# FFN opening product: every second weight unit as seven block products instead of eight

## The reference, cut to what matters

```python
h = rmsnorm(x, norm_ffn)                    # (512, 1024)
gt, up = jnp.split(h @ w_ffn_in, 2, axis=-1)  # w_ffn_in: (1024, 2 * 2816)
x = x + (jax.nn.silu(gt) * up) @ w_ffn_out  # w_ffn_out: (2816, 1024)
return rmsnorm(x, norm_final)
```

## Time and profile before

| what | value |
|---|---|
| runs of the kernel before | 799.06, 799.15, 800.95 us, median 799.15 |
| profiled execution | 799.31 us, its span 797.5 us |
| TensorE busy | 789.9 us of the span (99%) |
| VectorE, ScalarE, GpSimd busy | 406.2 us, 290.0 us, 24.8 us |
| granted TensorE clock, mean | 0.999 of full speed |
| HBM traffic | 75.34 MB read, 3.19 MB written |

### The profile page before, as it was taken

How to read it: one execution, slowest core, us unless ns; L and a number is a source line. 1 busy time by engine, 2 the same in 40 slices (tenths; PEclk the granted TensorE clock), 3 DMA queues, 4 the chain that set the end, 5 groups by cost and what they waited for, 6 DMA issues and landing times.

```text
span 797.5 us, 11178 instructions
## 1 busy us (share of the span) xinstructions
PE 789.9 (99%) x4382; PEld 659.1 (83%) x4382; DVE 406.2 (51%) x816; ACT 290.0 (36%) x524; POOL 24.8 (3%) x36
## 2 busy tenths in 40 slices
PE   9999999999999999999999999999999999999996
PEld 7878899889878787888889888888888888888885
DVE  5935333556766776656518533444433444422347
ACT  6112155243647666643317221222221223222235
POOL 1301000000000000003100000000000000000000
PEclk9999999999999999999999999999999999999999
DMA  7931354330311111164231333322333321222202
GB/s 236 345 116 53 106 102 137 83 110 4 106 53 54 54 55 41 40 185 133 105 106 54 106 105 105 102 77 84 105 105 105 102 87 75 106 105 105 105 1 106
DMA packets 100216, 79.08 MB, mean 99 GB/s; under 512 B 16929, under 2 KB 94801, under 8 KB 100177
## 3 DMA queue, kind: packets, MB, share of 16 engines
q1 hardware_dynamic: 99936, 78.26, 32.9%
q10 hardware_dynamic: 240, 0.29, 0.1%
HBM read 75.34 MB, written 3.19 MB: 98 GB/s over the span
## 4 chain that ended last, share of the span: by engine, by line
PE 99%; DMA 0%; ACT 0%; DVE 0%; issue 0%; ACTq 0%; DVEq 0%
PE bank L1451 28%; PE bank L1452 28%; PE bank L1453 28%; PE bank L1684 2%; PE bank L1703 2%; PE bank L1671 2%; PE bank L1585 1%; PE bank L1626 1%; PE bank L1607 1%; PE bank L1548 1%; PE bank L1475 1%; PE bank L1492 1%; PE bank L1698 1%; PE bank L1498 0%; PE bank L1501 0%; PE bank L1638 0%
## 5 line engine op out<-in xcount | busy, mean ns | idle before, releaser
L1451 PE MATMUL bank<-h_hi,w_hi 128*128 128x512 f32 (+1 forms) x368 | 140.0, 380 | 0.0
L1452 PE MATMUL bank<-h_lo,w_hi 128*128 128x512 f32 (+1 forms) x368 | 139.8, 380 | 0.0
L1453 PE MATMUL bank<-h_hi,w_lo 128*128 128x512 f32 (+1 forms) x368 | 139.8, 380 | 0.0
L1451 PE MATMUL bank<-n_hi,w_hi 128*128 128x512 f32 x272 | 108.8, 400 | 0.0
L1453 PE MATMUL bank<-n_hi,w_lo 128*128 128x512 f32 x272 | 106.1, 390 | 0.0
L1452 PE MATMUL bank<-n_lo,w_hi 128*128 128x512 f32 x272 | 106.0, 390 | 0.0
L889 DVE TENSOR_TENSOR w_lo<-w_raw,w_hi 128x2048 fp32r<-128x2048 f32 (+2 forms) x29 | 64.5, 2224 | 79.6 <-ACT w_hi L596 79.5
L1451 PEld LDWEIGHTS bank<-h_hi,w_hi 128*128 128x128 f32 x368 | 69.2, 188 | 13.1
L1453 PEld LDWEIGHTS bank<-h_hi,w_lo 128*128 128x128 f32 x368 | 69.2, 188 | 13.1
L1452 PEld LDWEIGHTS bank<-h_lo,w_hi 128*128 128x128 f32 x368 | 69.2, 188 | 12.9
L809 ACT ACTIVATE tanh_g<-gate_scaled 128x512 f32<-128x512 f32 x22 | 13.9, 632 | 180.4 <-DVE gate_scaled L1336 180.4
(11 more groups left out here) (222 smaller groups left out, 1162.6 us busy)
## 6 DMA issues: line engine op xcount, KB each, us to landing
w_raw<-in_w_ffn_in_dram SPq DMA_DIRECT2D x44, 512.0 KB, 4.6
w_raw<-in_w_in_dram SPq DMA_DIRECT2D x37, 512.0 KB, 4.8
w_raw<-in_w_ffn_out_dram SPq DMA_DIRECT2D x22, 512.0 KB, 3.8
w_raw<-in_w_out_dram SPq DMA_DIRECT2D x8, 512.0 KB, 3.7
w_raw<-in_w_in_dram SPq DMA_DIRECT2D x12, 256.0 KB, 4.5
xs<-in_x_dram SPq DMA_DIRECT2D x4, 512.0 KB, 5.0
wck_k<-in_w_ck_dram SPq DMA_DIRECT2D x1, 2048.0 KB, 11.8
wck_v<-in_w_cv_dram SPq DMA_DIRECT2D x1, 2048.0 KB, 14.7
```

The source lines that it names most:

```text
L1451: pe.matmul(dst, w[0], x_[0], start=start, stop=False)
L1452: pe.matmul(dst, w[0], x_[1], start=False, stop=False)
L1453: return pe.matmul(dst, w[1], x_[0], start=False, stop=stop)
```

## The change

Units 5, 7, ..., 19 (eight of the 22; `SEVEN_FROM = 5`, `SEVEN_N = 8`) are no longer multiplied as 2 halves x 8 chunks. Such a unit is a 2 x 2 grid of blocks (input rows 0 to 511 and 512 to 1023; gate and up), h is one too (input rows; tokens 0 to 255 and 256 to 511), and the product is made as seven products of blocks or of sums of blocks (Strassen's scheme in Winograd's form). Each is 4 chunks x 3 = 12 matmuls of 256 columns, so a unit has 84 of them. The units 0 to 4, the even ones and unit 21 stay as they are.

What is new around it:

- **Once:** four sums of blocks of h (`t7`, each 128 x 1024). One is made by three DVE operations, put between the small operations and the copy of the spread row. The other three are made by seven GpSimd operations in one chain, each waiting for the one before, which begins when `h_lo` is complete. ACT and DVE split all four into `thi` and `tlo` between units 2 and 3. `thi` lies where x2 lies, so x2 (2 MB) is written to DRAM before and read back behind the last seven-product unit.
- **Per unit:** GpSimd makes four sums of weight blocks (`weight_sums`, each 128 x 512) from `raw[1]`; ACT and DVE split the plain blocks (1024 and 512 values) and the sums (2048). DVE adds the block results (six additions of 256 columns that read a bank, and a scaling of 512), and ACT copies the first.
- The waits of PE inside a seven-product unit are for the ACT copy of m1 before the fifth product, for two DVE sums before the sixth and four before the seventh.
- The loops of PE, ACT and DVE run over a pair (seven-product unit, even unit).

```diff
+            pool.wait_ge(h_lo, 2 * TT)
+            link(pool.tensor_tensor(t_f[:, 2], h_f[:, second, late], h_f[:, first, late], ALU.subtract))
+            link(pool.tensor_tensor(t_f[:, 2], t_f[:, 2], l_f[:, second, late], ALU.add))
+            pool.tensor_tensor(t_f[:, 2], t_f[:, 2], l_f[:, first, late], ALU.subtract).then_inc(t_made, 1)
+            pool.wait_ge(t_made, 1)
...
+            def weight_sums(i, begins=False):
+                pool.wait_ge(raw_full[1], i * 32 + raw_count(U_IN + SEVEN_FROM))
+                if not begins:
+                    pool.wait_ge(lo_done, i * 2 + (U_IN + SEVEN_FROM - 1))
+                w = slot_view(raw, 1, KC, 256)
+                pool.tensor_tensor(s7[:, 2], w[:, 0:4, 0:P], w[:, 0:4, P:256], ALU.subtract).then_inc(s_sums, 1)
+                pool.tensor_tensor(s7[:, 0], w[:, 0:4, P:256], w[:, 4:8, P:256], ALU.add).then_inc(s_sums, 1)
+                pool.wait_ge(s_sums, i * 4 + 2)
+                pool.tensor_tensor(s7[:, 1], s7[:, 0], w[:, 0:4, 0:P], ALU.subtract).then_inc(s_sums, 1)
+                pool.wait_ge(s_sums, i * 4 + 3)
+                pool.tensor_tensor(s7[:, 3], w[:, 4:8, 0:P], s7[:, 1], ALU.subtract).then_inc(s_sums, 1)
...
             rsqrt(st[:, 1, 0:4], st[:, 1, 4:8], st[:, 3, 0:4], st[:, 3, 4:8], (r_ready, 2))
             link(dve.tensor_scalar(rhalf[:, 1, :], st[:, 3, 0:4], 0.5, None, ALU.mult))
+            t1 = t7[:, 0]
+            dve.tensor_tensor(t1, hhi[:, 0:4, 256:512].bitcast(F32), hhi[:, 0:4, 0:256].bitcast(F32),
+                              ALU.subtract).then_inc(t1_made, 1)
...
+            with dve.Fori(1, SEVEN_N - 1) as i:
+                even_act(i - 1)
+                up_to_u2(i)
+                up_to_u3(i)
+                even_lo(i)
+                three_blocks(i)
+                last_block(i)
+                plain_lo(i + 1)
+                seven_act(i)
+                sums_lo(i + 1)
...
+            with act.Fori(1, SEVEN_N - 1) as i:
+                even_tanh(i - 1)
+                keep_m1(i)
+                even_hi(i)
+                plain_hi(i + 1)
+                seven_tanh(i)
+                sums_hi(i + 1)
...
+                product(4, 0, plain(0, 4), turned(0, early))
...
+                product(5, 0, summed(1), mixed(1))
+                product(6, 0, summed(2), mixed(2))
+                product(7, 0, summed(0), mixed(0))
+                pe.wait_ge(m1_out, i + 1)
+                product(4, 256, plain(4, 8), turned(4, early))
+                pe.wait_ge(u_sums, i * 7 + 2)
+                product(6, 256, [v[1][:] for v in (ahi7, alo7)], mixed(3))
+                pe.wait_ge(u_sums, i * 7 + 4)
+                product(7, 256, summed(3), turned(4, late))
```

More of the change, by code:

```diff
@@ L36 @@
 FT = FF // P
+SEVEN_FROM = 5
+SEVEN_N = (FT - 1 - SEVEN_FROM) // 2
 CMP = 32
@@ L816, in _ @@
             tanh_gate(0, 1)
[L817 to L825, removed]
+            ffn_in(1, 0)
+            parts_of_t()
+            tanh_gate(1, 0)
+            ffn_in(1, 1)
+            plain_hi(0, True)
+            tanh_gate(1, 1)
+            sums_hi(0, True)
+            tanh_gate(2, 0)
+            keep_m1(0, True)
+            even_hi(0)
+            plain_hi(1)
+            seven_tanh(0)
+            sums_hi(1)
+            with act.Fori(1, SEVEN_N - 1) as i:
[5 more added lines that the diff above has]
+                sums_hi(i + 1)
+            even_tanh(SEVEN_N - 2)
+            keep_m1(SEVEN_N - 1)
+            even_hi(SEVEN_N - 1)
+            act.wait_ge(raw_full[1], raw_count(U_OUT - 1))
+            act.wait_ge(m_done, 7 * SEVEN_N)
+            act.copy(whi[1][:, 0:2048], raw[1][:, 0:2048]).then_inc(hi_done, 1)
+            seven_tanh(SEVEN_N - 1)
+            even_tanh(SEVEN_N - 1)
+            act.wait_ge(raw_full[0], raw_count(U_OUT))
+            act.wait_ge(gu_ready, SEVEN_N + SEVEN_FROM + 1)
+            act.copy(whi[0][:, 0:2048], raw[0][:, 0:2048]).then_inc(hi_done, 1)
+            act.copy(ahi[:, 0, :, :], actt[:, 0:2, :]).then_inc(a_hi, 1)
+            act.wait_ge(g_scaled, SEVEN_N + SEVEN_FROM + 1)
+            act.activation(tg[:, 1, :], gs[:, 1, :], ACT.Tanh, scale=0.5).then_inc(gu_tanh, 1)
             act.wait_ge(gu_free, 24)
@@ L1352, in _ @@
             ffn_in_act(0, 1)
[L1353 to L1363, removed]
+            ffn_in_lo(1, 0)
@@ new lines, in _ @@
+            parts_of_t(0)
+            parts_of_t(1)
+            ffn_in_act(1, 0)
+            ffn_in_lo(1, 1)
+            plain_lo(0)
+            ffn_in_act(1, 1)
+            sums_lo(0)
+            ffn_in_act(2, 0)
+            up_to_u2(0)
+            up_to_u3(0)
+            even_lo(0)
+            three_blocks(0)
+            last_block(0)
+            plain_lo(1)
+            seven_act(0)
+            sums_lo(1)
+            with dve.Fori(1, SEVEN_N - 1) as i:
[8 more added lines that the diff above has]
+                sums_lo(i + 1)
@@ new lines, in _ @@
+            even_act(SEVEN_N - 2)
+            up_to_u2(SEVEN_N - 1)
+            up_to_u3(SEVEN_N - 1)
+            even_lo(SEVEN_N - 1)
+            three_blocks(SEVEN_N - 1)
+            last_block(SEVEN_N - 1)
+            ffn_in_lo(FT // 2 - 1, 0)
+            seven_act(SEVEN_N - 1)
+            even_act(SEVEN_N - 1)
+            ffn_in_lo(FT // 2 - 1, 1)
+            dve.wait_ge(a_hi, 1)
+            dve.tensor_tensor(alo[:, 0, :, :], actt[:, 0:2, :], ahi[:, 0, :, :].bitcast(F32),
+                              ALU.subtract).then_inc(a_lo, 1)
@@ new lines, in _ @@
+            dve.wait_ge(gu_ready, SEVEN_N + SEVEN_FROM + 2)
+            dve.tensor_tensor(gs[:, 1, :], ps[2][:], rrow[:], ALU.mult).then_inc(g_scaled, 1)
+            dve.wait_ge(gu_tanh, SEVEN_N + SEVEN_FROM + 3)
+            dve.scalar_tensor_tensor(out=tm[:, 0, :], in0=tg[:, 1, :], scalar=1.0, in1=gs[:, 1, :],
+                                     op0=ALU.add, op1=ALU.mult).then_inc(gt_mul, 1)
+            dve.wait_ge(gt_mul, SEVEN_N + SEVEN_FROM + 3)
+            dve.tensor_tensor(actt[:, FT - 1, :], ps[3][:], tm[:, 0, :], ALU.mult).then_inc(gu_free, 1)
@@ L1838, in _, with seven, product, plain @@
             ffn_first()
[L1839 to L1842, removed]
+            def seven(i):
+                early, late = slice(0, 256), slice(256, 512)
+                def product(bank, c, w, x_):
+                    for k in range(4):
+                        ins = split_product(ps[bank][:, c:c + 256], [v[:, k, :] for v in w], [v[:, k, :] for v in x_],
+                                            k == 0, k == 3)
+                    ins.then_inc(m_done, 1)
+                def plain(lo, hi):
+                    return [v[0][:, lo:hi, :] for v in (ahi7, alo7)]
+                def summed(b):
+                    return [v[:, b] for v in (shi7, slo7)]
+                def turned(lo, tokens):
+                    return [v[:, lo:lo + 4, tokens] for v in (hhi, hlo)]
+                def mixed(b):
+                    return [v[:, b] for v in (thi, tlo)]
+                pe.wait_ge(wa_lo, i * 2 + 2)
+                pe.wait_ge(gu_free, i * 2 + (SEVEN_FROM + 1))
+                product(4, 0, plain(0, 4), turned(0, early))
+                pe.wait_ge(hi_done, i * 2 + (U_IN + SEVEN_FROM + 1))
+                pe.wait_ge(lo_done, i * 2 + (U_IN + SEVEN_FROM + 1))
+                product(5, 0, summed(1), mixed(1))
[7 more added lines that the diff above has]
+                product(7, 256, summed(3), turned(4, late))
+            ffn_in(0, 1, 2, lambda: spread_r(1, 4))
+            ffn_in(1, 0, 0)
+            ffn_in(1, 1, 2)
+            ffn_in(2, 0, 0)
+            pe.wait_ge(t_lo, 4)
+            with pe.Fori(0, SEVEN_N) as i:
+                seven(i)
+                ffn_in(i + (SEVEN_FROM + 1) // 2, 0, 0)
+            ffn_in(FT // 2 - 1, 1, 2)
             def ffn_out(s, tiles, first, last, ended=()):
```

155 lines of the change are left out of this document (147 added, 8 removed).

## The result

The changed kernel takes 805.16 us (median of 4 runs, 803.94 to 806.19) against 799.11 us: a ratio of 1.0069, 95% interval 1.0047 to 1.0092. It is slower by 6.05 us; 808.2 had been forecast, within 799 to 813. The profiled execution took 805.92 us, its span 804.1.

What follows compares the result with a forecast made beforehand. The prediction took TensorE to bound the kernel from end to end. Start delay +13.8, gain -6.8 and loop stalls +2.0 gave +9.0 us on the median of 799.15: 808.2 us, range 799 to 813 (the forecast's own 805 to 811).

Steps and rivals of the forecast that it cites:

- The gain per unit: Seven-product units: 84 narrow matmuls (10.03 us) replace 48 wide ones (10.88), 0.85 us less each, 6.8 in eight units.
- The exclusion at the start: FFN start: DVE operations with two SBUF operands and GpSimd operations exclude each other, delaying unit 2 by 13.8 us.
- A: First of GpSimd's seven operations on h: runs 436.55 to 439.0, ahead of DVE's w_lo, which waits until 439.0.
- B: Second of GpSimd's seven operations on h: waiting since 439.15, goes after DVE's w_lo, to 443.45.
- My doubling: GpSimd's 128x1024 operation on h taken as 2.44 us, from 1.29 for 128x512 with 0.14 of start.
- The clock: After its wait at the transposes PE runs for a time at 1.2 instead of 2.4 GHz, costing 1.7 us.
- The loop: Seven-product units: GpSimd's weight sums hold gate_mul and even_lo, a stall of 0.25 us in seven units, taken as 2.0.
- "none" for an earlier GpSimd: Lower bound of the loop's stall: no stall if GpSimd's weight sums come 0.7 us earlier.
- The 0.8 a unit for 0.5 later: Upper bound of the loop's stall: 0.8 us a unit (5.6) if GpSimd's weight sums come 0.5 later.
- The small operations did not slip by: Rival at the FFN start: 128x4 operations slip by, long sums still take turns; +3.8, 803 us; chance 0.18.
- That PE never waits: Rival at the FFN start: DVE seldom meets GpSimd, unit 2 is on time; 792.4, up to 794.5 us; chance 0.19.
- The third rival: Loop: third and fourth weight sums both precede even_lo, stall 1.6 us a unit, 11 in seven, 817 us; chance 0.03.

Runs made afterwards that it cites:

- e1: Changed kernel with GpSimd's seven sums of h replaced by three memsets that only write (three of h's four sums left out): 792.31 us, ratio 0.9911.
- e3: Changed kernel with GpSimd's chain of sums of h waiting for r_ready, behind the twelve small operations: 801.84 us, ratio 1.0032.
- e2: Changed kernel with GpSimd's seven sums of h as fourteen linked operations of half the length: 802.52 us, ratio 1.0036.
- e4: Changed kernel with GpSimd's chain waiting for unit 2's w_lo and the splits of the four sums behind unit 3's activation: 793.17 us, ratio 0.9924.
- e7: Changed kernel with all seven sums of h on VectorE, none on GpSimd, and the splits moved behind unit 3's activation: 792.61 us, ratio 0.9913.

## Why the prediction was right

Point by point, by its own steps.

- **The gain per unit.** 6.8 us forecast from the distance of the starts, 7.3 measured (7.4 in e1, where nothing is lost at the start). The sixty matmuls of the five products with a summed or mixed operand came at 0.1200, near the 0.1194 of the earlier trace rows; those of the first and fifth product, plain weights with plain h, at 0.1133 (below). Right, and slightly too small.
- **The exclusion at the start.** 13.8 forecast, 12.6 measured. The order was as worked out: A ahead of w_lo, B behind it, two small operations per gap, six GpSimd operations, then PE's transposes. The sizes: 2.34 to 2.41 us for a 128x1024 instead of 2.44, and 0.08 from one to the next instead of 0.15; r_ready at 457.42 - 1.66 = 455.8 counted from the kernel before's start, instead of 456.65. My doubling was 0.03 to 0.10 high. The estimate of 2.3 to 2.4 us from the 4497 ns at 2048 values in the Trainium skill (GPSIMD Engine Reference, section 3.1 Elementwise — side-by-side cycle accounting) was nearer; the trace agrees with it. That small operations with one input are held too is now shown: 2.37 for a 128x4 TENSOR_SCALAR in float32, 2.24 for one in int32, while the one between them came right behind a GpSimd operation and took 0.17. The Trainium skill (SBUF — State Buffer, section Who interferes with whom) says that a VectorE instruction with two SBUF inputs contends with a GpSimd one that reads SBUF and not with one that only writes it. The traces agree: w_lo took 3.98 us beside the first sum, and 2.29 beside the memsets of e1.
- **The clock.** PE stood idle from 447.2 on; the clock was granted at 0.50 (1.2 GHz) from 452 to 457. Behind the wait six matmuls took 2.66 us from start to start (458.24 to 460.90) instead of 1.36, and the transposes 0.76 instead of 0.35: 1.7 us, as forecast. As forecast it cost nothing, too: unit 2 had to wait for w_lo, which ended at 467.51 (465.22 + 2.29), while PE was through with unit 1 at 467.05. In e3 and e2 nothing hid it, and it cost 2.75 and 1.7 us.
- **The loop.** The one term that was wrong: 2.0 us forecast (0.25 in seven units), nothing measured. The step that failed is when things become ready in a pair. T is the start of a seven-product unit, here 521.22. I let the weights be there 5.2 us after the split and GpSimd begin at T+1.3, hold gate_mul with its first sum and even_lo with its third, the third 0.6 ahead of even_lo. Measured, its first sum begins 6.1 after the split (537.76 to 543.83), at T+1.8 (523.03), behind gate_mul at T+1.6 (522.80). Its third and even_lo then begin together at T+4.8, and even_lo wins. The picture that I drew is real: where GpSimd came just ahead of gate_mul (e2, e3, e4) it cost 0.42 a pair. Of the bounds, "none" for an earlier GpSimd fits the first pair (it began at T+0.7, no loss). The 0.8 a unit for 0.5 later did not: it came 0.5 later and cost nothing. That it cost nothing in all seven pairs was luck: in two of them GpSimd missed gate_mul by 0.01 us, and such distances the rows before could not give.
- **Rivals.** The small operations did not slip by (their rows). That PE never waits is refuted by 10.2 us; e1, e4 and e7 show the time it named, 792.4, once GpSimd's seven sums are gone from that place: 792.3, 793.2, 792.6. The third rival, both weight sums ahead of even_lo, was not seen in any run.

With 12.6 - 7.3 + 0 the sum is +5.3, with the forecast's terms +9.0: 1.2 from the start, 0.5 from the gain, 2.0 from the loop. All three errors point the same way. The direction and the cause were right by the forecast's own steps; that the time still lies inside its own 805 to 811, by 0.2 us, is luck: with the opening product's +5.3 alone it would be 804.5.

## What to carry to other kernels

Before work is given to an idle GpSimd, list what VectorE does beside it: every operation there with two SBUF operands, and a TENSOR_SCALAR too, stood still here and can stand still for the length of a GpSimd operation, so a chain of twelve tiny operations costs six long ones. The remedy was the place and not the engine's speed: the same chain begun 16 us later turned +6 us into -6. Work at the pace of starts shows in advance what a product saves; what it costs stands at its first use, where everything has to be prepared at once.

## What the hardware showed beside that

- Between two linked GpSimd operations lie 0.08 us. The small VectorE operation that waited ends with the first of them (445.06), and the next one (445.09) still gets in ahead of GpSimd's next (445.11); the third, 0.21 behind that one, has to wait. Two per GpSimd operation, with ones of 2.4 us and with ones of 1.3 us (e2).
- Hundredths of a microsecond decide who goes first. even_lo went ahead of the third weight sum in every pair in which the trace has both within 0.02 us (526.00). gate_mul was held where the first sum began 0.01 to 0.06 ahead of it, and not where it began at the same moment or later. What sets the outcome at a tie stays open.
- Matmuls of 256 columns of plain weight chunks with plain h start 0.1133 apart in a seven-product unit, those of the other five products 0.1200. The first matmuls of the first, the second, the fifth and the sixth product of one unit in the kernel after (12, 36 and 12 starts apart):

```profile
521.22 0.28 PE L1700 MATMUL bank<-h_hi,wa_hi 128*128 128x256 f32 x1
...
522.58 0.28 PE L1700 MATMUL bank<-t_hi,w_hi 128*128 128x256 f32 x1
...
526.90 0.28 PE L1700 MATMUL bank<-h_hi,wa_hi 128*128 128x256 f32 x1
...
528.26 0.28 PE L1700 MATMUL bank<-t_hi,wa_hi 128*128 128x256 f32 x1
```

Both sorts have the same shapes. Plain operands alone do not make the difference: unit 0, with plain weights and plain h too, came at 0.1194. Which of the operands' places does was not tried, and stays open.
